# Two layers of a mixed block and a third block in one kernel: the first unit of each feed-forward issued alone, and a new order of the first transfers and conversions

## What is computed

```python
for l in range(2):
    h = rmsnorm(x, g_mix[l]); proj = h @ w_in[l]
    ...                                  # four branches, gates
    x = x + mixed @ w_out[l]
    h = rmsnorm(x, g_ffn[l])
    gate, up = split(depthwise_conv3(h @ w_up[l]), 2)
    x = x + (silu(gate) * up) @ w_down[l]
...                                      # the second block: the same frame, other mixers
h = rmsnorm(x, norm_ffn_2)
a, u = split(h @ ffn_w_in_2, 2)
x = x + (gelu(causal_conv3(a)) * u) @ ffn_w_out_2
```

## Time and profile before

| | |
|---|---|
| median of 3 runs | 1458.65 us (1457.36 to 1459.93) |
| the profiled execution | 1458.64 us, of which the span of the profile is 1456.9 us |
| granted TensorE clock, mean | 0.997 of full |
| PE busy | 98% of the span |
| POOL busy | 81% |
| ACT / DVE busy | 61% / 49% |

### The profile page before, as it was taken

The page is one execution under the profiler, slowest core; times in us unless marked ns, Lnnn a source line. Parts: engine busy times, 40 slices in busy tenths (PEclk is TensorE's granted clock), DMA queues, the critical chain, the costliest instruction groups (busy, mean ns, idle before and its releaser), DMA issues.

```text
span 1456.9 us, 29053 instructions
## 1 busy us (share of the span) xinstructions
PE 1428.7 (98%) x9384; PEld 1292.4 (89%) x9384; DVE 709.3 (49%) x1605; ACT 883.8 (61%) x1499; POOL 1184.2 (81%) x926
## 2 busy tenths in 40 slices
PE   8999999999999999999999999999999999999998
PEld 7899998888878899987888889999899999888887
DVE  3653444555555733355545556670563542444444
ACT  5665645766666655647666666866445544755554
POOL 5877687999978776787999969899676799799985
PEclk9999999999999999999999999999999999999999
DMA  7654455666656554455665666556444465566662
GB/s 251 196 156 149 144 160 151 195 191 189 191 170 194 170 157 137 154 176 156 199 190 189 187 194 192 161 174 192 139 132 130 148 194 180 165 196 188 188 191 96
DMA packets 80037, 251.80 MB, mean 173 GB/s; under 512 B 7633, under 2 KB 22481, under 8 KB 79441
## 3 DMA queue, kind: packets, MB, share of 16 engines
q1 hardware_dynamic: 79088, 245.72, 54.6%
q10 hardware_dynamic: 864, 4.92, 1.0%
HBM read 249.56 MB, written 1.05 MB: 172 GB/s over the span
## 4 chain that ended last, share of the span: by engine, by line
PE 92%; ACT 3%; DVE 2%; issue 2%; DMA 0%; POOL 0%; SPq 0%; ACTq 0%; DVEq 0%; POOLq 0%
PE psum L959 21%; PE psum L960 20%; PE psum L961 20%; PE psum L991 16%; PE psum L993 8%; PE psum L1070 1%; PE psum L1136 1%; PE psum L1089 1%; ACT w_hi L436 1%; PE psum L1080 1%; PE psum L1058 0%; DMA raw<-in_units 0%; PE psum L1137 0%; PE psum L1097 0%; PE psum L1403 0%
## 5 line engine op out<-in xcount | busy, mean ns | idle before, releaser
L411 POOL TENSOR_TENSOR w_lo<-raw,w_hi 128x512 fp32r<-128x512 f32 x461 | 601.4, 1305 | 256.0 <-ACT w_hi L436 246.2
L412 POOL TENSOR_TENSOR w_lo<-raw,w_hi 128x512 fp32r<-128x512 f32 x461 | 608.2, 1319 | 0.0
L436 ACT ACTIVATE w_hi<-raw 128x1024 fp32r<-128x1024 f32 x461 | 486.0, 1056 | 187.7 <-PE psum L993 94.7
L959 PE MATMUL psum<-both,w_hi 128*128 128x256 f32 x1192 | 346.1, 290 | 2.3 <-POOL w_lo L412 2.3
L960 PE MATMUL psum<-both,w_lo 128*128 128x256 f32 x1192 | 337.5, 283 | 0.0
L961 PE MATMUL psum<-both,w_hi 128*128 128x256 f32 x1192 | 337.5, 283 | 0.0
L991 PE MATMUL psum<-both,w_hi 128*128 128x512 f32 x1040 | 259.3, 391 | 5.5 <-DVEq L1590 5.5
L959 PEld LDWEIGHTS psum<-both,w_hi 128*128 128x128 f32 x1192 | 228.7, 192 | 11.8 <-issue 8.5
L960 PEld LDWEIGHTS psum<-both,w_lo 128*128 128x128 f32 x1192 | 228.9, 192 | 0.3
L961 PEld LDWEIGHTS psum<-both,w_hi 128*128 128x128 f32 x1192 | 228.8, 192 | 0.0
L991 PEld LDWEIGHTS psum<-both,w_hi 128*128 128x128 f32 x1040 | 190.7, 188 | 42.6 <-POOL w_lo L412 4.6
(11 more groups left out here) (301 smaller groups left out, 2199.9 us busy)
## 6 DMA issues: line engine op xcount, KB each, us to landing
raw<-in_units SPq DMA_DIRECT2D x461, 512.0 KB, 3.5
arena<-in_consts ACTq DMA_DIRECT2D x1, 2320.0 KB, 9.0
arena<-in_bias ACTq DMA_DIRECT2D x2, 1024.0 KB, 4.8
arena<-in_consts SPq DMA_DIRECT2D x1, 1657.0 KB, 8.3
out<-arena SPq DMA_DIRECT2D x4, 256.0 KB, 2.7
pre<-in_x SPq DMA_DIRECT2D x2, 256.0 KB, 3.4
arena<-in_x SPq DMA_DIRECT2D x2, 256.0 KB, 4.7
prm<-in_params ACTq DMA_DIRECT2D x2, 153.5 KB, 2.6
```

What stands on the lines that cost most here:

```text
L411: pool.tensor_tensor(w_lo[s][:, 0:D // 2], raw[s][:, 0:D // 2], w_hi[s][:, 0:D // 2].bitcast(F32), ALU.subtract)
L412: pool.tensor_tensor(w_lo[s][:, D // 2:D], raw[s][:, D // 2:D], w_hi[s][:, D // 2:D].bitcast(F32), ALU.subtract)\
L436: act.activation(w_hi[s][:, :], raw[s][:, :], ACT.Copy).then_inc(hi_ready, d.inc(hi_ready))
L959: pe.matmul(out, hi, r_hi, start=start, stop=False, **kw)
```

## The change

Four edits.

1. In `feed_forward` the first two units no longer share the loop over the chunks. The first runs alone in the loop, with its waits for `hlo_ready` and the turn behind chunk 1; the second follows as an `up_unit`, which issues its eight 512-column matmuls and then its eight 256-column ones without waits between them.
2. For the first layer the load of `prm` is issued as ScalarE's first instruction, ahead of its wait for `init`, and no longer behind the first root. The other two loads of parameters stay where they were.
3. `norm` has a place for conversions between the second root and the chunks of h (`beside`). In the first layer one unit is converted there, and two instead of three behind the chunks.
4. The load of `consts1` leaves out the columns ahead of `cos` (1778 of 3314), which the kernel fills itself or does not read.

```diff
-            sp.dma_start(arena[:, A1["consts"]:A1["consts"] + NK1], t["consts1"]).then_inc(...)
+            sp.dma_start(ck("cos", 0, NK1 - K1["cos"]), t["consts1"][:, K1["cos"]:]).then_inc(...)
...
-            def norm(load, gain, ahead=0, new_params=False):
+            def norm(load, gain, ahead=0, new_params=False, beside=0):
                 root_mean_square(load)
+                high(beside)
...
             d.skip(unit_done, RING)
+            act.dma_start(prm[:, :], t["params1"][0]).then_inc(params_full, d.inc(params_full))
             act.wait_ge(init, d.next(init))
             for layer in range(DEPTH):
                 def load_params1():
 
-                    act.dma_start(prm[:, :], t["params1"][layer])\
-                        .then_inc(params_full, d.inc(params_full))
                     if layer == 0:
                         high()
-
-                norm(load_params1, P1["g_mix"], 2 if layer else 3, True)
+                    else:
+                        act.dma_start(prm[:, :], t["params1"][layer]).then_inc(params_full, d.inc(params_full))
+
+                norm(load_params1, P1["g_mix"], 2, True, 0 if layer else 1)
...
             def feed_forward(n):
 
 
-                pair = []
-                for _ in range(2):
-                    pair.append((unit(), next_slot()))
-                    pe.wait_ge(slot_free, d.next(slot_free))
+                s, k = unit(), next_slot()
+                pe.wait_ge(slot_free, d.next(slot_free))
                 for c in range(CH):
                     pe.wait_ge(hlo_ready, d.next(hlo_ready))
-                    for s, k in pair:
-                        pe.matmul(bank(4 + k), blocks_of(w_hi[s], c), both[:, 2 * c * T:2 * (c + 1) * T], ...)
-                        last = pe.matmul(slot(k), blocks_of(w_lo[s], c), chunk(h_hi, c), ...)
-                        if c == CH - 1:
-                            last.then_inc(unit_done, d.inc(unit_done))
+                    pe.matmul(bank(4 + k), blocks_of(w_hi[s], c), both[:, 2 * c * T:2 * (c + 1) * T], ...)
+                    last = pe.matmul(slot(k), blocks_of(w_lo[s], c), chunk(h_hi, c), ...)
+                    if c == CH - 1:
+                        last.then_inc(unit_done, d.inc(unit_done))
                     if c == 1:
                         pe.wait_ge(x_ready, d.next(x_ready))
                         turn_raw(1, range(4, CH)).then_inc(turned, d.inc(turned))
+                up_unit()
                 pe.wait_ge(root_rows, d.next(root_rows))
```

More of the change, by code:

```diff
@@ L366, in _ @@
                 load_group(0, RING + s, s)
-            sp.dma_start(arena[:, A1["consts"]:A1["consts"] + NK1], t["consts1"]).then_inc(consts1_full, d.inc(consts1_full))
+            sp.dma_start(ck("cos", 0, NK1 - K1["cos"]), t["consts1"][:, K1["cos"]:]).then_inc(consts1_full, d.inc(consts1_full))
             for layer in range(DEPTH):
@@ L1126, in feed_forward @@
             def feed_forward(n):
-                pair = []
-                for _ in range(2):
-                    pair.append((unit(), next_slot()))
-                    pe.wait_ge(slot_free, d.next(slot_free))
+                s, k = unit(), next_slot()
+                pe.wait_ge(slot_free, d.next(slot_free))
                 for c in range(CH):
                     pe.wait_ge(hlo_ready, d.next(hlo_ready))
-                    for s, k in pair:
-                        pe.matmul(bank(4 + k), blocks_of(w_hi[s], c), both[:, 2 * c * T:2 * (c + 1) * T], start=(c == 0), stop=False, skip_group_check=True)
-                        last = pe.matmul(slot(k), blocks_of(w_lo[s], c), chunk(h_hi, c), start=False, stop=(c == CH - 1), skip_group_check=True)
-                        if c == CH - 1:
-                            last.then_inc(unit_done, d.inc(unit_done))
+                    pe.matmul(bank(4 + k), blocks_of(w_hi[s], c), both[:, 2 * c * T:2 * (c + 1) * T], start=(c == 0), stop=False, skip_group_check=True)
+                    last = pe.matmul(slot(k), blocks_of(w_lo[s], c), chunk(h_hi, c), start=False, stop=(c == CH - 1), skip_group_check=True)
+                    if c == CH - 1:
+                        last.then_inc(unit_done, d.inc(unit_done))
                     if c == 1:
```

## The result

| | before | changed |
|---|---|---|
| median (9 runs each) | 1458.61 us | 1462.08 us |
| lowest to highest | 1456.76 to 1459.93 | 1458.73 to 1463.61 |
| ratio, 95% interval | | 1.0022, 1.0012 to 1.0033 |
| profiled execution (span) | 1458.64 (1456.9) | 1462.40 (1460.6) |

The changed kernel is slower by 0.22%, with an interval for the ratio that lies clear of 1 and reaches to both sides of 0.2%. My 1459.6 was 2.5 us too low. The range (1457.0 to 1462.2) holds the result with 0.1 us to spare, and the result lies above 1461.6, where I had put only 0.17 of the chances.

The account below looks back on a forecast made before the run. TensorE, busy for 98% of the span, was taken to bound the kernel, so only its waits counted. 1458.6 - 3.8 (start) + 4.8 (three feed-forwards) = 1459.6 us, range 1457.0 to 1462.2.

Parts of the forecast that it names:

- 0.17 of the chances: Whole kernel: slower than 1461.6 us, through the clock, the start without gain and half of the port.
- the whole start: First layer's start, edits 2 to 4: -4.0 for unit 1's gap, +0.2 for edit 2, -3.8 us together.
- the 1.56 us of half clock: Start, unit 1: 15 matmuls at half clock behind the 2.43 us wait cost 3.36 us instead of 1.80.
- The 0.4 us that I took for a later x: Start, edit 2: the `prm` transfer ahead of x delays x by 0.4 us, bounds 0 and 0.5.
- the rival of the port: Start: GpSimd's second unit holds off VectorE's diagonal by 1.27 or 2.5 us, giving 1460.9 or 1462.1; chance 0.10.
- the transfer's own pace: Start, edit 4: 889 of 1657 KB less means 4.4 us less queue ahead of unit 8, costed at nothing.
- 1.6 forecast: Each feed-forward, edit 1: the roots' matmuls start 1.6 us later; counted three times, 4.8 us.
- the same pattern to a few hundredths: Feed-forward: the other two stages were said to match the first, so its 1.6 us counts three times.
- the step "Sum": Whole kernel: 1458.6 - 3.8 + 4.8 = 1459.6 us; all bounds one way, 1458.6 to 1460.3.
- the clock: Feed-forward rival: gaps between chunks halve the clock, 1.56 us each of three times, giving 1464.3; chance 0.07.
- three of TensorE's waits: Waits taken to bear on the change: 5.5 us for slots, 4.0 for GpSimd's low parts, 1.5 for first h chunks.
- my 1.0: Whole kernel: forecast net loss, from -3.8 us at the start and +4.8 us in the feed-forwards.

Follow-up runs that it names:

- factors first: Changed kernel with the roots' matmuls (factors) moved between the first and the second unit: 1456.04 us, ratio 0.9974 to the kernel before.
- changed in both series: The changed kernel with all four edits, measured twice: 1462.08 us (ratio 1.0022), and again beside the experiments 1461.89 us (ratio 1.0021).
- chunk gaps filled: Changed kernel with 7 unused matmuls of zeros between the chunks of h in each feed-forward: 1461.63 us, ratio 1.0016 to the kernel before.
- the pair: Kernels with the first two units side by side in the chunk loop, without edit 1; edits 2 to 4 so: 1455.28 us (0.9969), again 1455.81 (0.9978).
- the wait filled: Edits 2 to 4 with two units side by side, plus 16 unused matmuls before TensorE's wait for the slots: 1455.36 us, ratio 0.9964.

## Why the prediction was right, and where it was off

*The start, edit 3.* Right in each term for the profiled execution: conversion in ScalarE's idle time, low part at 16.90 (17.0 forecast), no half clock, L1206 at 28.34 (28.5). Forecast for the whole start -3.8, measured 3.92 in the profiles and 0.22% to 0.31% of 1459, 3.2 to 4.5 us, in the medians of the two runs of edits 2 to 4. Undoing edit 3 undoes all of it. But I took the 1.56 us of half clock as certain. They are not, as is shown below.

*Edit 2.* The 0.4 us that I took for a later x is not there; the mistake was to read the bound from the queue's share as a delay of x. VectorE's diagonal took 0.88 as before and ended at 14.48, while GpSimd's next instruction is shown from 14.39. The conversion ended at 14.31, just ahead of GpSimd's first unit at 14.39 and not 0.1 behind it as I had read from the rows. So the condition that I had set for the rival of the port was met, and still VectorE was not held for another half: the rival is refuted in this profile, and in all others the instruction stayed between 0.87 and 0.88.

*Edit 4.* Right that it gives only margin, but its size was too large: 2.1 us of margin at unit 8 (3.7 less 1.6), where the transfer's own pace gave 4.4.

*The feed-forward, edit 1.* Right in mechanism and nearly in size: 1.6 forecast, 1.51 to 1.54 measured, with the roots' matmuls 7.9 us behind the first. The wait for the slots is 2.15 only in the first two stages; in the third it is 1.17, before and after, which I had passed over with "the same pattern to a few hundredths". It changes nothing, since there too TensorE waits for the chain behind `factors`. The experiment with factors first shows that the cost passes through ScalarE's wait there.

*What was off* is the step "Sum": it had no term for the clock. I gave the clock 0.07, placed it in the gaps between the chunks, and set against it that one wait of over 2 us kept 1.00. That was one sample of something that comes and goes: 9 of 20 such waits have a fall behind them, at 1.57 us each. The same profile of the kernel before had a fall behind 1.99 us (844.50, shown above). The prediction doesn't mention it: it took three of TensorE's waits and left out the 4.2 us for the low part of f. I had named "if the clock leaves 1.00 near the feed-forwards" as a sign of being wrong, and it came. So it was in part luck that the range held: it had room for spread, not for this. The Trainium skill, TensorE: Matmul & The Clock Gate, "HAM oscillation — how this bites in real kernels", describes how a wait between stretches of matmuls brings the half clock back each time; the trace agrees that it comes behind waits, but here it came behind fewer than half of those of 2.15 us.

*The median.* Every run has its mean granted clock on record, to three digits. A fall takes 1.7 us of clock (0.43 of each of two windows of 2 us, as shown above) out of a span of 1457 us, or 0.0012 of the mean, so a run that reads 1.000 had none. Three things follow.

- Of the 97 runs of the kernel before beside the experiments, 22 read 1.000. In these its start had the wait but no half clock behind it, and there edit 3 had 2.4 us to give and not 4.0.
- Of the 41 runs with edit 1 and the wait for the slots left as it is (edit 1 alone, changed in both series, chunk gaps filled), none reads 1.000. On the chip where both sorts ran most, it is 0 of 24 against 16 of 47 with the pair. So falls are likelier with edit 1. The profiles point to the second feed-forward: a fall behind its wait for the slots in 4 of 4 with edit 1, in 1 of 6 with the pair.
- Within one kernel, 0.001 less of mean clock goes with 1.1 us more (an estimate, from a fit over all runs). Taken at equal clock, edit 1 costs 4.3 us against the kernel before and 4.9 against edits 2 to 4, and the changed kernel stands 1.9 us over the kernel before (interval 1.5 to 2.5) where the means of its second series differ by 2.7. The local terms without the start's half clock give 4.57 - 2.36 = 2.2.

So some 2 us of the changed kernel's loss are local, and my 1.0 was too small because it credited the start with a half clock that is not always there. The rest goes with a lower clock.

*What stays open.* Why edit 1 makes the falls likelier is not shown; it isn't the gaps between the chunks, since filling them left 0 of 12 runs at 1.000. At equal clock edits 2 to 4 stand 2.9 to 3.3 us under the kernel before, 0.6 to 0.9 more than the local 2.36; the fit is rough, since the clock is rounded and takes in the end of the span, where TensorE is idle.

## What to carry to other kernels

When an engine follows a producer chunk by chunk, a second piece of independent work in the same loop is what hides the producer's pace; move it behind the loop and the whole of it lands in front of whatever waits for the loop's end. Before putting work behind a signal, look at who is idle for that signal (ScalarE's 0.72 us here). An idle engine's wait is the place for a conversion that another engine needs early: one call moved gave 3.9 us in the profile. Edits 2 to 4 with the pair kept are 0.2% to 0.3% under the kernel before, and with the wait filled 0.36%, which can't be told apart. Before counting a stretch at half clock as part of a gain or leaving it out of a sum, look whether other executions have it: the mean clock of many runs tells that where one profile can't.

## What the runs showed of the hardware that was not expected

In otherwise dense work the clock fell behind 9 of 20 waits of 2.15 us and 11 of 28 waits of 1.99 us, and behind none of the waits of 0.73 and 1.17 us; 16 matmuls of zeros in the wait kept it at 1.00 in 6 of 6. The same kernel ran with and without falls: the mean clock of the kernel before read from 0.995 to 1.000, and its time from 1456.0 to 1464.1 us. The arrival of x, from the same six transfers, moved the start by up to 1 us from one kernel's profile to another (8.47 to 9.46 with the same first instructions).
